# The order of attention units and the place of their loads in a fused transformer layer on one core

## The chip, the cores and the metric

The kernel runs on one core of a Trainium2 chip. The metric is the device time of one execution in microseconds (us), and lower is better. Five engines run side by side, each with its own instruction stream, and meet at semaphores: TensorE (PE; PEld is its weight load), VectorE (DVE), ScalarE (ACT), GpSimd (POOL) and SyncE (SP, which here only issues DMAs and waits).

## The reference

One layer of a diffusion transformer over 1024 latent tokens and 256 context tokens, width 1024: a modulated norm, one combined input projection, two groups of attention heads side by side, an output projection, and then a mixture of experts (top 8 of 64, and one shared expert). The part at issue is attention. There are four differential heads, each with two score matrices, whose probabilities are subtracted, and eight grouped query heads, which share two key heads.

```python
def mix_groups(dq, dk, dv, gq, gk, gv, lam, lam_init, subln_g):
    o1 = attend(dq[:, :, :, 0], dk[:, :, :, 0], dv, sc)
    o2 = attend(dq[:, :, :, 1], dk[:, :, :, 1], dv, sc)
    o_diff = rmsnorm(o1 - lam.astype(o2.dtype) * o2, subln_g) * (1.0 - lam_init)
    o_gqa = attend(gq, gk, gv, sc)
    return jnp.concatenate([o_diff.reshape(b, L, -1), o_gqa.reshape(b, L, -1)], axis=-1)
```

`attend` is plain softmax attention of 1024 queries over 1280 keys (context and latent); all is float32.

## The kernel before

Three functions follow one another on all engines: `front` (modulation, projections), `attention`, `tail` (output projection, routing, experts). Queries and keys are split into a high and a low part; `front` writes them to HBM scratch (`q_scratch`, `k_scratch`), and `attention` loads them from there. Key heads 0 to 7 are the differential ones, 8 and 9 the grouped ones.

**Units.** Attention is cut into 24 units. A differential unit ("d", block, head) takes 512 queries of one head, with 8 score rows of 128 queries (two for each tile, as there are two score matrices). A grouped unit ("g", tile, key head) takes 128 queries of the four query heads that share a key head, with 4 rows. The order (L716 to L719) is: four differential, eight grouped, four differential, eight grouped. `row0[u]` counts the rows ahead of unit u.

**The pipeline.** While unit u is in its body, ten steps kt of turning probabilities (`tr`, L1084) and multiplying them by the values (`pv`, L1098 and L1102), TensorE also scores the rows of unit u+1 (`qk`, L1070) at steps that `ROW_AT` names; at the end of the body it scores row 0 of unit u+2 and, for a differential one, row 1 as well. Each row goes from TensorE to VectorE (`rowmax`, L975) to ScalarE (`exp`, L933). The rows of unit 0 and the first of unit 1 are scored ahead of the loop (L1116 to L1119). Grouped rows lie at columns 0 and 1280 of the score banks, so both parities use the third bank, and the last 256 columns of a row wait for the row before (L1067). At the end of a body ScalarE copies the sum (`out_o`, L948) and TensorE turns it back (`back`) in step 1 of the next body; then VectorE's `finish(u)` (L999) scales it into one of two output tiles `ob`. From unit 2 on `finish` waits for the store of unit u-2 (L1002). The product of step 1 waits for `finish` (L1096). For a differential unit Pool does half of the subtractions (`mix`, L881).

**Loads and stores.** Pool issues, in its own order, four query loads a unit (`load_q`, double buffered, after the rows of the unit two before are scored) and one load for each key head (640 KB). Heads 0 and 1 lie in `k_first`, loaded near the end of `front` together with the first queries; the other eight lie in `k_high_low`. `s_k` has one semaphore for each pair of key heads. SP issues, in its own order: the load of the sub-norm's gain; then it waits for all five key semaphores (L843); then six transfers for later stages (L845 to L850: constants, 257 KB of pads, 4 MB of zeros from HBM to HBM, the first 3 MB of w_out); then the output stores of the units one after the other, each when its unit is ready. Ahead of unit 18's turn it loads the rest of w_out and the first output tile (L853 to L859).

Of the kernel before, what the change touches and what calls it, by code (L numbers as in the profile page):

```python
# [19 lines left out]
P = 128  # L20
D = 1024
KD = D // P
SEQ, CTX = 1024, 256
NT, NC = SEQ // P, CTX // P
# [3 lines left out]
DH, GH, GKV = 4, 8, 2  # L28
# [58 lines left out]
def load_queries(eng, s_q, dst, q_d, h0, nh, at, w):  # L87

    for part in range(2):
        for r in range(2):  # L90
            eng.dma_start(dst[r * HD:(r + 1) * HD, part, 0:nh * w].rearrange("p (c n) -> p c n", n=w),
                          q_d[part, h0:h0 + nh, :, at:at + w].rearrange("c d n -> d c n")).then_inc(s_q, 16)


def load_key(eng, s_k, dst, k_d, hd):

    eng.dma_start(dst, k_d[hd].rearrange("e d n -> (e d) n")).then_inc(s_k[hd // 2], 16)


def front(b, a, ident, rows, nlam, mhalf, vv, first, s_q, s_k, q_d, k_d):  # L100
# [10 lines left out]
    units = [(c, t) for c in range(len(CH)) for t in ORDER if t >= NC or CH[c][2] != "q"]  # L111
    NU = len(units)
    heads = {"k": 8, "kv": 2, "v": 0, "q": 8}
    turned = [n for n in range(NU) if heads[CH[units[n][0]][2]]]
    normed = [n for n in range(NU) if CH[units[n][0]][3] == 8]
    last_of = [max(n for n in range(NU) if units[n][0] == c) for c in range(len(CH))]
    first_of = [min(n for n in range(NU) if units[n][0] == c) for c in range(len(CH))]
# [35 lines left out]
    with ExitStack() as ph:  # L153
# [11 lines left out]
        qk = b.sb(ph, "qk_rows", [P, 2, 512])  # L165
# [74 lines left out]
        @block.gpsimd  # L240
        def _(pool):
            nc.gpsimd.memset(mhalf[:, 0:16], -0.5)
            nc.gpsimd.memset(mhalf[:, 16:32], EPS).then_inc(s_pool, 1)
            pool.wait_ge(s_pool, 1)
            n = [1]

            def rstd(dst, src, w, done):
                nc.gpsimd.tensor_tensor(dst, src, mhalf[:, 16:16 + w], ALU.add).then_inc(s_pool, 1)
                n[0] += 1
                pool.wait_ge(s_pool, n[0])  # L250
                nc.gpsimd.tensor_tensor(dst, dst, mhalf[:, 0:w], ALU.pow).then_inc(done, 1)

            for i, t in enumerate(XORDER):
                if i == 4:
                    pool.dma_start(rt[:], a["k_rope"][CTX:].rearrange("(t p) a d -> p t a d", p=P)).then_inc(s_rt, 16)
                    pool.dma_start(gain[:, 0], a["q_norm_g"].broadcast_to([P, HD])).then_inc(s_rt, 16)
                    pool.dma_start(gain[:, 1], a["k_norm_g"].broadcast_to([P, HD])).then_inc(s_rt, 16)
                pool.wait_ge(s_sq, i + 1)
                rstd(ssq[:, 1, t:t + 1], ssq[:, 0, t:t + 1], 1, s_rx)
            for r, g in ((G1, "g_post_mix"), (A2, "g_pre_ffn"), (G2, "g_post_ffn")):  # L260
                pool.dma_start(rows[:, r], a[g].broadcast_to([P, D])).then_inc(s_gains, 16)
            for m in range(NU):
                if m in normed:
                    nh = heads[CH[units[m][0]][2]]
                    pool.wait_ge(s_hv, n_normed(m) + 1)
                    rstd(hss[:, m % 2, 1, 0:nh], hss[:, m % 2, 0, 0:nh], nh, s_rr)
            qf, kf = first
            pool.wait_ge(s_wl, len(CH) * KD)
            pool.wait_ge(s_mt, NM)
            pool.wait_ge(s_mm, EARLY + 4 * (NM - EARLY))  # L270
            for hd in range(2):
                load_key(pool, s_k, kf[:, hd], k_d, hd)
            ready = turned.index(first_of[-1] + 4)
            for u in range(2):
                pool.wait_ge(s_st[u], stored(u, ready))
            load_queries(pool, s_q[0], qf, q_d, 0, 2, 0, 512)

        @block.sync
        def _(sp):
# [427 lines left out]
def attention(b, a, ident, rows, nlam, mhalf, moe, wa, vv, first, s_q, s_k, q_d, k_d, o_d, rows_d, slot_d, y2_d, early, s_od):  # L707
# [4 lines left out]
    NKH = 10  # L712
    QB = 4
    KEEP = 5

    units = []  # L716
    for qb in range(SEQ // (QB * P)):
        units += [("d", qb, p) for p in range(DH)]
        units += [("g", qb * QB + t, h) for t in range(QB) for h in range(GKV)]  # L719
    NU = len(units)  # L720

    def n_rows(u):
        return 8 if units[u][0] == "d" else 4
# [22 lines left out]
    def mixes(u, pool):  # L746
        return [i for i in range(4) if (i in ON_POOL) == pool] if units[u][0] == "d" else []
# [30 lines left out]
    with ExitStack() as ph:  # L778
        qf, kf = first
# [42 lines left out]
        S = psS[:].rearrange("p b n -> p (b n)")  # L822

        def key(hd):
            return kf[:, hd] if hd < 2 else k2[:, hd - 2]

        def pT(u, kt):
            return psS[:, 5 + turn_bank(u, kt)]
# [2 lines left out]
        @block.sync  # L831
        def _(sp):
            def store(u):
                kind, t, p = units[u]
                sp.wait_ge(s_o, u + 1)
                if kind == "d":
                    sp.dma_start(o_d[t * QB * P:(t + 1) * QB * P, p * DIFF_V:(p + 1) * DIFF_V].rearrange("(t p) n -> p t n", p=P),
                                 ob[:, u % 2].rearrange("p (t n) -> p t n", n=P)).then_inc(s_od[u % 2], 16)
                else:
                    sp.dma_start(o_d[t * P:(t + 1) * P, 512 + p * 256:512 + (p + 1) * 256], ob[:, u % 2, 0:256]).then_inc(s_od[u % 2], 16)  # L840

            sp.dma_start(sg[:], a["subln_g"].broadcast_to([P, DIFF_V])).then_inc(s_g, 16)
            for w in s_k:  # L843
                sp.wait_ge(w, 32)
            sp.dma_start(rows_d, rows[0:1].rearrange("p r n -> p (r n)")).then_inc(s_later, 16)  # L845
            sp.dma_start(slot_d, a["k_pads"]).then_inc(s_later, 16)
            sp.dma_start(y2_d[0:SEQ, :], a["k_zeros"]).then_inc(s_later, 16)
            sp.dma_start(first_row[:], a["k_first"].broadcast_to([P, E])).then_inc(s_later, 16)
            sp.dma_start(token[:], a["k_token"]).then_inc(s_later, 16)
            sp.dma_start(wa[:], a["w_out"][0, 0:wa.shape[1] * P, :].rearrange("(k p) n -> p k n", p=P)).then_inc(s_later, 16)  # L850
            last_diff = max(u for u in range(NU) if units[u][0] == "d")
            for u in range(NU):
                if u == last_diff + 3:  # L853
                    sp.wait_ge(s_s, row0[last_diff + 1])
                    sp.dma_start(w_rest[:], a["w_out"][0, wa.shape[1] * P:, :].rearrange("(k p) n -> p k n", p=P)).then_inc(s_rest, 16)
                    for w in s_od:
                        sp.wait_ge(w, (DH + GKV) // 2 * 16)
                    sp.dma_start(o_first[:], o_d[0:P, :]).then_inc(s_of_tile, 16)
                    sp.dma_start(x_first[:], a["tokens"][CTX:CTX + P, :]).then_inc(s_xr, 16)  # L859
                if u >= 1:  # L860
                    store(u - 1)
            store(NU - 1)
            sp.wait_ge(s_later, 96)
            sp.wait_ge(s_before, 16)
# [7 lines left out]
        @block.gpsimd  # L872
        def _(pool):
            def load_q(u):
                kind, t, p = units[u]
                if u >= 2:
                    pool.wait_ge(s_s, row0[u - 1])
                w, h0, nh, at = (512, 2 * p, 2, t * 512) if kind == "d" else (P, 2 * DH + 4 * p, 4, t * P)
                load_queries(pool, s_q[u % 2], (qf, qs)[u % 2], q_d, h0, nh, at, w)

            def mix(u, i):  # L881
                n = n_mix[u] + i
                m = n_mixp[u] + mixes(u, True).index(i)
                B = pb[:, i % 2]
                A = pr[:, u % 2, i]
                pool.wait_ge(s_c, n + 1)
                nc.gpsimd.tensor_scalar(B, B, cs[:, n % 4, 1:2], None, ALU.mult).then_inc(s_cs, 1)
                pool.wait_ge(s_cs, m + 1)
                nc.gpsimd.tensor_tensor(A, A, B, ALU.add).then_inc(s_mixp, 1)

            def rstd(u):
                pool.wait_ge(s_ov, n_diff[u] + 1)
                nc.gpsimd.tensor_tensor(ms[:, 2], ms[:, 1], mhalf[:, 0:4], ALU.pow).then_inc(s_or, 1)

            load_key(pool, s_k, key(2), k_d, 2)
            load_q(1)
            load_key(pool, s_k, key(3), k_d, 3)
            for i in mixes(0, True):
                mix(0, i)
            for hd in range(4, NKH):  # L900
                load_key(pool, s_k, key(hd), k_d, hd)
            nc.gpsimd.memset(ones[:], 1.0)
            pool.dma_start(before[:], a["k_before"]).then_inc(s_before, 16)
            for u in range(1, NU + 2):
                if u + 1 < NU:
                    load_q(u + 1)
                if u >= 2 and units[u - 2][0] == "d":
                    rstd(u - 2)
                if u < NU:
                    for i in mixes(u, True):  # L910
                        mix(u, i)
# [144 lines left out]
        def _(pe):  # L1056
# [59 lines left out]
            for r in range(n_rows(0)):  # L1116
                qk(0, r)
            qk(1, 0)
            qk(1, 1)  # L1119

            def second_row_late(u):
                return units[u][0] == "g"
# [1134 lines left out]
```

## Time and profile before

| what | us |
|---|---|
| median of three runs | 2174.56 (2169.73 to 2176.85) |
| span of the profiled execution | 2171.7 |
| projections and what is ahead of them | 0 to 372.2 |
| attention | 372.2 to about 889 |
| output projection, routing, experts, sum | about 889 to 2171.7 |

| engine | busy us of the span | share |
|---|---|---|
| PE | 1988.6 | 92% |
| PEld | 1487.5 | 68% |
| DVE | 1574.7 | 73% |
| ACT | 1351.4 | 62% |
| POOL | 942.6 | 43% |

The shares are means over stages that differ. The mean granted clock of TensorE is 0.971 of full speed; a value of 0.50 in a window is 1.2 GHz, 1.00 is 2.4 GHz. In a row of the timeline the first number is the start in us from the span's start, the second the length, and the bracket tells how long the engine was idle before it and what released it.

### The profile page before, as it was taken

To read this page: it belongs to the slowest core of one execution; us is meant where nothing else is said; L and a number is where in the kernel's file an instruction comes from. 1 tells how busy PE (TensorE), PEld (TensorE's weight loads), DVE (VectorE), ACT (ScalarE), POOL (GpSimd) and SP (SyncE) were. 2 spreads that over 40 slices of the span, in tenths; PEclk is the share of its full clock that TensorE was granted. 3 is DMA by queue.
4 is the path that set the end of the run, shared out by engine and by line. 5 is a ranking of instruction groups with operands and counts; after the bars stand their busy time and mean duration, and the time that the engine had idled before them with its cause. 6 is when DMAs were issued, how large, how long until landed. Compare 5 with 4: busy or idle time off the path is not lost.

```text
span 2171.7 us, 36325 instructions
## 1 busy us (share of the span) xinstructions
PE 1988.6 (92%) x9592; PEld 1487.5 (68%) x9592; DVE 1574.7 (73%) x2206; ACT 1351.4 (62%) x1952; POOL 942.6 (43%) x869
## 2 busy tenths in 40 slices
PE   4899998888988899989889999999999999999993
PEld 2676666555656566676548888888877888888881
DVE  3752374685556655465539999999988999999985
ACT  2421121555656556423338998999878999899982
POOL 1000011661135410044435666666656666666663
PEclk8999998799999999999999999999999999999997
DMA  7464346732122121397249998889999977789957
GB/s 266 140 181 141 98 145 160 218 80 42 40 50 41 40 78 30 113 192 155 80 129 320 327 368 285 244 259 330 354 333 351 343 234 229 217 233 366 287 147 260
DMA packets 162652, 429.18 MB, mean 198 GB/s; under 512 B 26993, under 2 KB 82033, under 8 KB 137889
## 3 DMA queue, kind: packets, MB, share of 16 engines
q1 hardware_dynamic: 92818, 294.36, 38.0%
q0 software_dynamic: 60048, 116.89, 24.2%
q10 hardware_dynamic: 9712, 16.99, 2.7%
q8 instruction: 41, 0.67, 0.1%
q14 instruction: 33, 0.27, 0.0%
HBM read 360.83 MB, written 96.26 MB: 210 GB/s over the span
## 4 chain that ended last, share of the span: by engine, by line
PE 43%; DMA 7%; DVE 3%; issue 2%; ACT 2%; ACTq 1%; POOL 0%; SPq 0%; DVEq 0%; POOLq 0%
PE ps_d L2099 11%; PE ps_r L2082 7%; PE ps_r L2084 7%; PE ps_r L2083 7%; DMA w_experts<-in_w_exp_down 5%; PE ps_y L2072 3%; PE ps_y L2001 2%; PE ps_g L2020 2%; PE ps_d L2039 1%; DMA x_in<-in_tokens 1%; PE ps_g L2106 1%; ACT w_gate_up_high L1612 1%; ACTq L1321 1%; DVE w_gate_up_low L1844 1%; PE ps_d L2001 1%
## 5 line engine op out<-in xcount | busy, mean ns | idle before, releaser
L1844 DVE TENSOR_TENSOR w_gate_up_low<-w_experts,w_gate_up_high 128x1024 fp32r<-128x1024 f32 x416 | 489.3, 1217 | 20.1 <-ACT w_gate_up_high L1612 20.0
L1612 ACT ACTIVATE w_gate_up_high<-w_experts 128x1024 fp32r x416 | 416.6, 1050 | 38.0 <-SPq L1366 17.4
L2082 PE MATMUL ps_r<-w_gate_up_high,gatheredT_high 128*128 128x512 f32 x832 | 335.2, 403 | 5.5 <-DVE gatheredT_low L1850 5.4
L1501 POOL DMA_INDIRECT y_scratch<-e_y,e_target_index x104 | 281.4, 2705 | 108.5 <-POOL e_target_index L1497 93.0
L2084 PE MATMUL ps_r<-w_gate_up_high,gatheredT_low 128*128 128x512 f32 x832 | 326.1, 392 | 0.0
L2083 PE MATMUL ps_r<-w_gate_up_low,gatheredT_high 128*128 128x512 f32 x832 | 324.2, 390 | 0.0
L975 DVE TENSOR_REDUCE neg_max<-ps_scores 128x1 f32<-128x1280 f32 x128 | 190.2, 1490 | 182.5 <-PE ps_scores L1070 182.4
L1879 DVE TENSOR_TENSOR w_down_low<-w_experts,w_down_high 128x2048 fp32r<-128x2048 f32 x103 | 236.0, 2292 | 44.8 <-ACT w_down_high L1637 44.1
L1487 POOL DMA_INDIRECT gathered<-h_scratch,e_gather_index x106 | 197.2, 1860 | 95.2 <-POOL e_gather_index L1484 90.1
L1637 ACT ACTIVATE w_down_high<-w_experts 128x2048 fp32r x103 | 198.0, 1923 | 36.1 <-issue 36.1
L933 ACT ACTIVATE probs<-ps_scores,neg_max 128x1280 f32<-128x1280 f32 x96 | 127.5, 1329 | 102.1 <-DVE neg_max L975 102.0
L1084 PE MATMUL ps_scores<-ident,probs 128*128 128x128 f32 x960 | 149.4, 283 | 38.0 <-ACT probsT L942 21.6
L2082 PEld LDWEIGHTS ps_r<-w_gate_up_high,gatheredT_high 128*128 128x128 f32 x832 | 156.6, 188 | 38.4 <-issue 9.4
L2084 PEld LDWEIGHTS ps_r<-w_gate_up_high,gatheredT_low 128*128 128x128 f32 x832 | 156.4, 188 | 34.3
L1084 PEld LDWEIGHTS ps_scores<-ident,probs 128*128 128x128 f32 x960 | 108.3, 143 | 101.4 <-ACT probsT L942 61.9
L2083 PEld LDWEIGHTS ps_r<-w_gate_up_low,gatheredT_high 128*128 128x128 f32 x832 | 157.0, 189 | 29.8 <-issue 0.2
L942 ACT ACTIVATE probsT<-ps_scores 128x512 f32<-128x512 f32 x192 | 112.5, 594 | 89.6 <-PE ps_scores L1084 89.6
L681 PE MATMUL ps_chunk<-w_in_high,hT_high 128*128 128x512 f32 (+1 forms) x368 | 143.9, 391 | 9.0 <-DVE hT_low L522 7.3
L1658 ACT ACTIVATE e_y<-ps_d 128x512 f32<-128x512 f32 x208 | 122.3, 592 | 38.6 <-PE ps_d L2099 37.4
L2099 PE MATMUL ps_d<-w_down_high,e_actT_high 128*128 128x512 f32 x416 | 137.9, 413 | 1.9 <-DVE e_actT_low L1868 1.8
L681 PE MATMUL ps_chunk<-w_in_high,hT_low 128*128 128x512 f32 (+1 forms) x368 | 136.9, 372 | 0.0
L681 PE MATMUL ps_chunk<-w_in_low,hT_high 128*128 128x512 f32 (+1 forms) x368 | 136.6, 371 | 0.0
(294 smaller groups left out, 3824.1 us busy)
## 6 DMA issues: line engine op xcount, KB each, us to landing
w_experts<-in_w_exp_gate SPq DMA_DIRECT2D x64, 1024.0 KB, 9.4
w_experts<-in_w_exp_up SPq DMA_DIRECT2D x64, 1024.0 KB, 13.0
w_experts<-in_w_exp_down SPq DMA_DIRECT2D x64, 1024.0 KB, 17.3
w_mod_later<-in_w_mod ACTq DMA_DIRECT2D x32, 512.0 KB, 3.7
w_mod_first<-in_w_mod SPq DMA_DIRECT2D x4, 2048.0 KB, 15.4
w_in_raw<-in_w_in SPq DMA_DIRECT2D x32, 256.0 KB, 3.6
values<-in_tokens SPq DMA_DIRECT2D x10, 512.0 KB, 11.3
k_high_low<-k_scratch POOLq DMA_DIRECT2D x8, 640.0 KB, 7.2
```

The costliest lines, as they stand in the source:

```text
L681: last = nc.tensor.matmul(psC[:, n % 4, 0:w], H[:, k, tok], W[:, m % WR, 0:w], start=(k + i == 0), stop=(k == KD - 1 and i == 2))
L1084: last = nc.tensor.transpose(pT(u, kt)[:, j * P:(j + 1) * P], pr[:, u % 2, j, kt * P:(kt + 1) * P], ident[:])
L1487: pool.indirect_dma_start(xg[u][:], None, h2_d, bass.IndirectOffsetOnAxis(ap=gi[u][:, 0:1], axis=0), bounds_check=SEQ - 1, oob_is_err=Fals ...
L1501: pool.indirect_dma_start(y_d[u], bass.IndirectOffsetOnAxis(ap=si[u][:, 0:1], axis=0), ye[u][:], None, bounds_check=SEQ + P - 1, compute_o ...
L1612: act.activation(split_slice(eH, j), raw_slice(ring, slot, j), ACT.Copy).then_inc(X["wH"], 1)
L1637: act.activation(dh[:].rearrange("p k n -> p (k n)"), ring[:, ds(slot, 1), 4096:6144].rearrange("p o n -> p (o n)"), ACT.Copy).then_inc(X[ ...
L1844: nc.vector.tensor_tensor(split_slice(eL, j), raw_slice(ring, slot, j), split_slice(eH, j).bitcast(F32), ALU.subtract).then_inc(X["wL"], 1)
L1879: nc.vector.tensor_tensor(dl[:].rearrange("p k n -> p (k n)"), ring[:, ds(slot, 1), 4096:6144].rearrange("p o n -> p (o n)"), dh[:].rearra ...
L2082: nc.tensor.matmul(psR[:], xH[:, k], eH[:, k], start=(k == 0), stop=False)
L2083: nc.tensor.matmul(psR[:], xH[:, k], eL[:, k], start=False, stop=False)
L2084: last = nc.tensor.matmul(psR[:], xL[:, k], eH[:, k], start=False, stop=(k == KD - 1))
L2099: last = nc.tensor.matmul(psD[:, h], A[:, k], W[:, k, h * 512:(h + 1) * 512], start=(j + k == 0), stop=(j + k == 3))
```

## The change

The first eight grouped units (tiles 0 to 3) come first, then all eight differential units, then the other eight grouped ones. So the loads near the end of the projections become the queries of grouped unit 0 (four heads, 128 columns) and key heads 8 and 9, which now lie in `k_first`; the eight differential key heads lie in `k_high_low` and are loaded two at a time in Pool's turns u = 1 to 4, each time behind the queries of unit u+1. Row 1 of unit 1 is no longer scored ahead. The wait ahead of the first output tile's load is for units 0 to 11.

```diff
@@ front, gpsimd
-            for hd in range(2):
-                load_key(pool, s_k, kf[:, hd], k_d, hd)
-            ready = turned.index(first_of[-1] + 4)
+            ready = turned.index(first_of[3]) + 1
             for u in range(2):
                 pool.wait_ge(s_st[u], stored(u, ready))
-            load_queries(pool, s_q[0], qf, q_d, 0, 2, 0, 512)
+            load_queries(pool, s_q[0], qf, q_d, 2 * DH, 4, 0, P)
+            for hd in range(2 * DH, 2 * DH + GKV):
+                load_key(pool, s_k, kf[:, hd - 2 * DH], k_d, hd)
@@ attention
-    units = []
-    for qb in range(SEQ // (QB * P)):
-        units += [("d", qb, p) for p in range(DH)]
-        units += [("g", qb * QB + t, h) for t in range(QB) for h in range(GKV)]
+    grouped = [("g", t, h) for t in range(NT) for h in range(GKV)]
+    differential = [("d", qb, p) for qb in range(SEQ // (QB * P)) for p in range(DH)]
+    units = grouped[:QB * GKV] + differential + grouped[QB * GKV:]
     NU = len(units)
+    TILE0 = QB * GKV + DH
...
-            return kf[:, hd] if hd < 2 else k2[:, hd - 2]
+            return k2[:, hd] if hd < 2 * DH else kf[:, hd - 2 * DH]
...
-                        sp.wait_ge(w, (DH + GKV) // 2 * 16)
+                        sp.wait_ge(w, TILE0 // 2 * 16)
...
-            load_key(pool, s_k, key(2), k_d, 2)
             load_q(1)
-            load_key(pool, s_k, key(3), k_d, 3)
-            for i in mixes(0, True):
-                mix(0, i)
-            for hd in range(4, NKH):
-                load_key(pool, s_k, key(hd), k_d, hd)
             nc.gpsimd.memset(ones[:], 1.0)
             pool.dma_start(before[:], a["k_before"]).then_inc(s_before, 16)
             for u in range(1, NU + 2):
                 if u + 1 < NU:
                     load_q(u + 1)
+                if u <= DH:
+                    for hd in (2 * u - 2, 2 * u - 1):
+                        load_key(pool, s_k, key(hd), k_d, hd)
...
             for r in range(n_rows(0)):
                 qk(0, r)
             qk(1, 0)
-            qk(1, 1)
```

## Rows read from the trace of the kernel before

**Rows 1.** Windows: busy us (instructions) of five engines; clock, DMA share, GB/s.
```profile
404.00:408.00 4.00, 3.54 (x13) 2.74 (x11) 1.28 (x1) 1.79 (x4) 0.06 (x1) 0.50 1.11 419
...
540.00:560.00 20.00, 19.54 (x113) 12.39 (x112) 9.85 (x10) 11.97 (x20) 2.75 (x5) 1.00 0.27 53
658.00:665.00 7.00, 6.31 (x19) 4.39 (x18) 2.38 (x5) 3.17 (x7) 2.49 (x1) 0.51 0.05 19
```

**Rows 2.** Timeline, start of attention: start, length, engine, line, operation [idle <- releaser].
```profile
369.24 0.51 SPq L309 DMA_DIRECT2D q_scratch<-turned_low  x1
...
372.42 4.61 PE L1070 MATMUL ps_scores<-k_first,q_first 128*128 128x512 f32 x12 [5.06 <-PEq L153]
...
377.41 1.33 ACT L933 ACTIVATE probs<-ps_scores,neg_max 128x1280 f32<-128x1280 f32 x1 [9.33 <-DVE neg_max L975]
...
383.01 1.33 ACT L933 ACTIVATE probs<-ps_scores,neg_max 128x1280 f32<-128x1280 f32 x1 [2.78 <-DVE neg_max L975]
...
397.71 3.31 POOL L97 DMA_DIRECT2D k_high_low<-k_scratch  x6
...
401.69 1.05 PE L1084 MATMUL ps_scores<-ident,probs 128*128 128x128 f32 x4
```

**Rows 3.** Timeline of ScalarE: the copies that end units 0 to 4.
```profile
430.29 0.60 ACT L948 ACTIVATE oT_head<-ps_out 128x512 f32<-128x512 f32 x1
...
458.13 0.59 ACT L948 ACTIVATE oT_head<-ps_out 128x512 f32<-128x512 f32 x1
...
485.98 0.59 ACT L948 ACTIVATE oT_head<-ps_out 128x512 f32<-128x512 f32 x1
...
511.31 0.59 ACT L948 ACTIVATE oT_head<-ps_out 128x512 f32<-128x512 f32 x1
...
527.97 0.59 ACT L948 ACTIVATE oT_head<-ps_out 128x512 f32<-128x512 f32 x1
```

**Rows 4.** Timeline, one grouped body among its like (560.17 to 576.27).
```profile
560.17 0.59 ACT L948 ACTIVATE oT_head<-ps_out 128x512 f32<-128x512 f32 x1
...
562.95 0.17 DVE L1003 RECIPROCAL row_scale<-row_sum 128x4 f32<-128x4 f32 x1
...
565.28 1.08 PE L1102 MATMUL ps_out<-probsT,values 128*64 128x512 f32 x4
...
568.32 1.43 PE L1070 MATMUL ps_scores<-k_high_low,q_first 128*128 128x512 f32 x6
...
570.04 2.45 POOL L91 DMA_DIRECT2D q_first<-q_scratch  x4 [13.65 <-PE ps_scores L1070]
...
576.27 0.59 ACT L948 ACTIVATE oT_head<-ps_out 128x512 f32<-128x512 f32 x1
```

**Rows 5.** Timeline of SP: first and last of its bundle, and the first output store.
```profile
412.66 0.24 SPq L845 DMA_DIRECT2D rows_scratch<-mod_rows  x1
...
415.33 0.56 SPq L850 DMA_DIRECT2D w_out_ahead<-in_w_out  x1
...
446.84 0.38 SPq L837 DMA_DIRECT2D o_scratch<-o_tile  x1
```

**Rows 6.** Windows while the bundle moves; the last two columns are DMA share and GB/s.
```profile
418.00:422.00 4.00, 4.00 (x23) 3.18 (x23) 1.84 (x2) 2.70 (x6) 3.92 (x2) 1.00 1.55 508
...
426.00:430.00 4.00, 4.00 (x16) 2.38 (x15) 3.93 (x5) 2.10 (x3) 0.79 (x2) 1.00 0.06 14
...
442.00:444.00 2.00, 2.00 (x9) 1.04 (x8) 1.97 (x3) 1.51 (x2) 1.92 (x2) 1.00 0.38 135
```

**Rows 7.** Landing times: six key loads (L97, from 397.7), then seven grouped stores (L840).
```profile
DMA to landing us min/median/max: 4.4/7.2/12.1
...
DMA to landing us min/median/max: 1.7/1.7/1.9
```

**Rows 8.** DMA queues in 430 to 444 (q1 is SP's, q0 Pool's): packets, MB, share.
```profile
q1 hardware_dynamic: 885, 3.13, 74.0%
q0 software_dynamic: 576, 1.05, 25.5%
```

## The prediction

> **What bounds the kernel now.** I read the windows by stage first, for what the change can reach: the last few us of the projections and all of attention. In the grouped units TensorE is busy 19.5 us of 20 at the full clock (2.4 GHz) [rows 1], so there the pitch is TensorE's own work. In the differential units it shares the pace with the chain scores, row maximum, exponential. Then I read the timeline of the start of attention: the last query store is issued at 369.24, the first scores start at 372.42, and until 401.69 (the first turn of probabilities, L1084) the engines only fill the pipeline: 29.3 us in which a row's maximum and exponential wait for one another [rows 2]. Third, the copies of the finished output (oT_head, L948), one a unit: their distance is the length of a unit's body. A differential unit followed by another takes 27.84 us (458.13 to 485.98), one followed by a grouped unit 25.33, a grouped unit right after a differential one 16.66 [rows 3], a grouped unit among its like 16.10 (560.17 to 576.27) [rows 4]. Last I read SP's issues and the DMA windows, because the change moves what SP waits for [rows 5, 6].
>
> **Part 1, the loads inside the projections: nothing.** Pool issues four query loads (128 KB each in place of 256 KB) and the two grouped keys where it issued two keys, and no longer loads queries at 356. Pool was free for them at 339.9; the last key is then issued at 343 and in by 355 even at the slowest landing, 12.1 [rows 7], 17 us ahead of the first scores at 372.42 [rows 2]. They share engines with SP's query stores there, each of which has two projection chunks before its buffer is wanted. If this cover failed, a store of 2.5 us would come late once: 1 to 2 us. The end of the projections hangs on the last rotary step and the last two stores, and neither moves. In attention Pool starts with load_q(1) at once; its memset and the load of "before" come earlier, beside idle Pool time.
>
> **Part 2, the fill: about -11.9 us.** Before, eight rows of unit 0 and two of unit 1 are scored ahead, and Pool mixes probabilities; now four and one. The first exponential starts at 377.41 and ends 1.33 later, at 378.74 [rows 2]; this stays, since it waits on the same things. Grouped rows share their third score bank, so the last 256 columns of a row wait for the exponential of the row before: the chain is serial, 1.49 (maximum) + 1.33 (exponential) + about 0.5 (two 256-column products at half clock, from 4.61 us for twelve products of 5120 columns [rows 2]) + 0.15 of handing over = 3.5 us a row. Three more rows end at 389.2, and the last piece of unit 1's row makes the first turn start at 389.8 in place of 401.69. A differential pair came in 5.6 us (377.41 to 383.01 [rows 2]), so the bounds for three rows are 8.4 and 10.8: -11.0 to -14.0. The second row of unit 1, no longer scored ahead, is scored after the first turn as in every other grouped body.
>
> **Part 3, the first body: about -9.5 us.** Unit 0 took 430.29 - 401.69 = 28.6 us; a grouped one takes 16.10 at full clock. The granted clock was 0.50 at 404 to 408 although TensorE was busy [rows 1], and a TensorE-bound body feels that: each us at 1.2 GHz costs half a us. Nothing to 11 us of it costs 0 to 5.5; I take 3, so 19.1 us: -9.5, bounds -7 to -12.5.
>
> **Part 4, the order: about +13.7 us.** Both orders hold the same 24 units. The new one has two more bodies of differential followed by differential (because the first unit, counted in part 3, is now a grouped one), and one less of differential-to-grouped and of grouped-after-differential: 2 x 27.84 - 25.33 - 16.66 = +13.7 [rows 3]. The way from grouped to differential is paid once in both. TILE0 makes SP await six stores a parity in place of three, but still in unit 18, when units 0 to 11 are long stored: nothing. Parts 2 to 4 together: -7.7 us.
>
> **Part 5, the keys one pair a unit: a new wait, about +28.4 us.** This is where the change is paid. Before Pool had issued the last keys by 401 (six from 397.71 [rows 2]), SP woke at 412.66 and issued the zeros, the row constants and the 3 MB of w_out by 415.9; the first output store came much later, at 446.84 [rows 5], when the queue was empty. Now heads 6 and 7 are loaded in Pool's turn u = 4, behind load_q(5), which waits for the last row of unit 3. SP waits for ALL keys before its bundle, and **every output store stands behind that wait on SP**. VectorE's finish of unit 2 (L1001 to L1002) needs the store of unit 0, as the output tile has two buffers, and it runs early in unit 3's body. Count from the start of unit 2's body, which is the copy of unit 1's output:
> - the last row of unit 3 is scored and Pool released at 570.04 - 560.17 = +9.87 [rows 4]
> - four query loads, 2.45, and the first key, 0.6 (six took 3.31 [rows 2]): the second key is issued at +12.9
> - landing 6.0: the quickest of the six keys took 4.4, the median 7.2 [rows 7]: keys are in at +18.9
> - SP's bundle, in the transfer order of its queue: from 412.6 to 430 it moved pads, zeros, then only small rows at 14 GB/s; w_out, issued at 415.33, moved only from 430 [rows 5, 6] and ended about 443.5, where the engines' share falls to 0.38 [rows 6]. In that stretch SP's queue had 74.0% of the transfers and Pool's queries 25.5% [rows 8]; now no queries go out meanwhile, so 3.13 MB at the 300 to 330 GB/s of both together is 10 us in place of 13.5: 27.4, and 31 without that saving
> - the store's own landing, 1.7 [rows 7], plus its start: store of unit 0 in at about +48.9 (30 after the keys)
> - needed: unit 3's body starts at +16.1; finish starts 2.78 into it and the product L1102, which waits for it, 5.11 into it; the finish takes 0.6, so 1.6 us are slack [rows 4]: +20.5
> The stall is 48.9 - 20.5 = **28.4 us**. Bounds: with keys landing after 4.4 and the bundle in 28.5, 25.3; with 12.1 and 33, 37.5. Queued behind VectorE's wait are the row maxima of unit 4, thus ScalarE's exponentials and TensorE's turns; TensorE stops at L1102 for want of the freed output bank, and Pool's next loads wait for its rows. Later waits for stores find them landed: they pay nothing again.
>
> The Trainium skill has two rules here. "DMA: Bandwidth & Descriptors", section "Queues, rings and completion order", says an engine takes turns between queues packet by packet; by it w_out alone goes at the full rate, the 27.4 above. The trace agrees in the shares of rows 8. The same section says completion within one issuing engine is not first in, first out; a store that used this would land early, which is the first rival below. The trace speaks for order here: w_out waited 15 us behind the rest [rows 5, 6].
>
> **Part 6, the clock after the stall: about +3.5 us.** TensorE idles some 25 us, then has 11 us of unit 3's body left, all its own work. After pauses the trace shows half clock for 7 us (658 to 665) and, in the fill, up to 412 [rows 1]: 4 to 11 us at 1.2 GHz, 2 to 5.5 us lost.
>
> **Sum.** -11.9 - 9.5 + 13.7 + 28.4 + 3.5 = +24.2 us. The profiled span of 2171.7 becomes 2195.9; the median of the runs stands 2.9 above that span, so 2198.8 us, 1.1% slower. The rest (output projection, experts) starts later and is otherwise as it was. A measurement of this kernel can tell about 0.3%, 6.5 us, from no change.
>
> **The rivals.**
> - *The store slips past the bundle* (the other side). If SP's 128 KB store lands 1.7 after its issue though 7 MB are queued ahead, it is in at 18.9 + 3.3 + 1.7 = +23.9, and VectorE waits 3.4 us, with little loss of clock. Then -7.7 + 3.4 = -4.3: 2170.3; and if the first body also runs at full clock, -7.3: 2167. It decides for faster once the store comes under +22 and the first body loses under 2 us. Against it: w_out did not pass the zeros [rows 5, 6]. Chance 0.07, of which 0.03 is faster.
> - *The wait is not there at all*, because SP is released before unit 2: -7.7, 2166.9. It needs the last keys in by about unit 0; Pool's wait for row scores puts them two units later. Chance 0.02.
> - *A shorter stall*: zeros and w_out drain without contention in 20 us, not 30: +14, 2188.6. For it: at 418 to 422 the engines moved 508 GB/s [rows 6]. Against: the 4 us of small rows at 14 GB/s [rows 6]. Chance 0.10.
> - *A longer stall*: keys and queries compete as in the 12.1 us landing [rows 7], or the zeros go slower: +33 to +38, 2208 to 2213. Chance 0.13.
> - *The forecast*, 2192 to 2206: 0.68.
>
> **How the numbers follow.** The likeliest case gives 2198.8. The low end takes in most of the shorter stall, 2188; the high end is the upper bounds of part 5 with the rest as taken, 2211. Faster: 0.03 + 0.02 = 0.05. Same: 0.04 and a bit of the shortest stalls, 0.05. Slower: 0.90.
>
> **What would show it.** Right: the first turn L1084 near 390 and the first copy L948 near 409; copies then 16.1 apart until unit 3, whose body is some 48 us long; SP's first issue after the last key lands, about 444; a VectorE idle of about 28 us before L1003, put down to a store to o_scratch; a granted clock of 0.5 in and just after it; then 27.8 for six differential bodies in a row. Wrong: stores landing in 2 us while w_out is moving; VectorE's wait absent; grouped bodies other than 16.1 before unit 3; or a change beyond attention's last copy.

## The result, and the profile after

The changed kernel takes 2197.48 us (median of four runs, 2191.74 to 2203.39), the kernel before 2173.23 (four runs, 2169.73 to 2176.85): a ratio of 1.0101, with a 95% interval of 1.0079 to 1.0124. It is 1.0% slower. The forecast was 2198.8 (2188 to 2211). The profiled span grew from 2171.7 to 2193.5 us, by 21.8.

Line numbers of attention are three lower than before: the scores are L1067 (was L1070), the turns L1081 (L1084), the grouped product L1099 (L1102), the copy that ends a unit L945 (L948), the first step of `finish` L1000 (L1003).

First the waits of the changed kernel from 372 to 500 (who waited for whom: us in total, times, longest). In the trace of before neither engine waits for a store of the output between 372 and 520.

```profile
DVE row_scale L1000 <- DMA o_scratch<-o_tile: 27.2, 1, 27.2
PE ps_out L1099 <- DVE o_tile L1009: 25.6, 1, 25.6
```

One wait of VectorE, 27.2 us, put down to a store to `o_scratch`; one of TensorE behind it, 25.6 us. Now the copies that end the units, from ScalarE's timeline: units 0, 1, 2, 3 and the last.

```profile
412.09 0.59 ACT L945 ACTIVATE oT_head<-ps_out 128x512 f32<-128x512 f32 x1
...
428.18 0.59 ACT L945 ACTIVATE oT_head<-ps_out 128x512 f32<-128x512 f32 x1
...
444.27 0.59 ACT L945 ACTIVATE oT_head<-ps_out 128x512 f32<-128x512 f32 x1
...
487.99 0.59 ACT L945 ACTIVATE oT_head<-ps_out 128x512 f32<-128x512 f32 x1
...
909.61 0.60 ACT L945 ACTIVATE oT_head<-ps_out 128x512 f32<-128x512 f32 x1 [1.28 <-PE ps_out L1099]
```

Units 1 and 2 take 16.09 us each, as grouped bodies did in rows 4; unit 3 takes 43.72, which is 27.6 too long; no later body differs from its like in the kernel before by more than 2.3 us. The timeline of SP and of what it holds up, from 447 on:

```profile
447.73 0.24 SPq L845 DMA_DIRECT2D rows_scratch<-mod_rows  x1
...
450.40 0.47 SPq L850 DMA_DIRECT2D w_out_ahead<-in_w_out  x1
...
450.91 40.89 SPq L840 DMA_DIRECT2D o_scratch<-o_tile  x4
474.29 0.18 DVE L1000 RECIPROCAL row_scale<-row_sum 128x4 f32<-128x4 f32 x1 [27.16 <-DMA o_scratch<-o_tile]
...
475.07 1.98 PE L1099 MATMUL ps_out<-probsT,values 128*64 128x512 f32 x4 [25.63 <-DVE o_tile L1009]
```

In rows 5 SP began its bundle at 412.66, and the first store went out long after it, at 446.84. Here the bundle starts at 447.73 and the store of unit 0, ready since about 415.5, is issued right behind it, at 450.91. The landing time of that one store, and then of the two keys issued at 440.5 and 441.0:

```profile
DMA to landing us min/median/max: 23.3/23.3/23.3
...
DMA to landing us min/median/max: 4.2/5.4/6.5
```

23.3 us, where rows 7 have 1.7 to 1.9 for such a store: it lands at 474.2, and VectorE goes on at 474.29. And what the DMA engines did meanwhile (windows; columns as in rows 1):

```profile
456.00:460.00 4.00, 0.00 (x0) 0.00 (x0) 0.00 (x0) 0.00 (x0) 0.00 (x0) 0.50 1.36 442
460.00:464.00 4.00, 0.00 (x0) 0.00 (x0) 0.00 (x0) 0.00 (x0) 0.00 (x0) 0.50 0.16 55
...
468.00:472.00 4.00, 0.00 (x0) 0.00 (x0) 0.00 (x0) 0.00 (x0) 0.00 (x0) 0.50 1.02 421
```

No compute engine does anything; the queue moves the zeros (to about 461), then little until about 464 (55 GB/s in the second window, which still holds the zeros' end: the small rows), then w_out at 421 GB/s, then the store. Which transfer a window belongs to is inferred from the order of issue; experiments 3 and 4 test it by taking the large ones out. It is the sequence of rows 6, with the store at its end.

### The profile page after: what moved, and what is told of

Same layout as the page of the kernel before. It is cut to its first block, busy times and chain, and to the rows that moved or that the text cites. A ratio compares the mean times of both kernels' runs of the same rounds, so it can differ in the third digit from the quotient of the medians.

```text
span 2193.5 us, 36328 instructions
## 1 busy us (share of the span) xinstructions
PE 1990.6 (91%) x9592; PEld 1485.8 (68%) x9592; DVE 1579.7 (72%) x2206; ACT 1350.9 (62%) x1952; POOL 944.2 (43%) x869
## 4 chain that ended last, share of the span: by engine, by line
PE 42%; DMA 7%; issue 3%; DVE 3%; ACT 2%; ACTq 1%; SPq 0%; POOL 0%; DVEq 0%; POOLq 0%
PE ps_d L2095 10%; PE ps_r L2078 7%; PE ps_r L2080 7%; PE ps_r L2079 7%; DMA w_experts<-in_w_exp_down 5%; PE ps_y L2068 3%; PE ps_y L1997 2%; PE ps_g L2016 2%; PE ps_d L2035 2%; PE ps_d L1997 1%; ACT w_gate_up_high L1608 1%; DMA x_in<-in_tokens 1%; ACTq L1317 1%; PE ps_g L2102 1%; DVE w_gate_up_low L1840 0%
## 5 line engine op out<-in xcount | busy, mean ns | idle before, releaser
L1081 PE MATMUL ps_scores<-ident,probs 128*128 128x128 f32 x960 | 149.1, 283 | 35.1 <-ACT probsT L939 18.2
L1081 PEld LDWEIGHTS ps_scores<-ident,probs 128*128 128x128 f32 x960 | 108.4, 143 | 96.8 <-ACT probsT L939 55.0
```

What stands on the lines that cost most here:

```text
L1081: last = nc.tensor.transpose(pT(u, kt)[:, j * P:(j + 1) * P], pr[:, u % 2, j, kt * P:(kt + 1) * P], ident[:])
```

## The experiments

All ratios are to the kernel before, run on the same chip in the same job. Two theories stood against each other: that VectorE waited for a store which stood behind SP's key wait and its bundle, and that the grouped-first order, or the late bundle as such, costs by itself.

**1. Two stores ahead of the bundle.** The changed kernel; SP awaits the keys and issues the six transfers in its turn 3, behind the stores of units 0 and 1. (The cut is abridged: "..." stands for the wait and the six transfers.)

```diff
-            for w in s_k: ...                # key wait and six transfers, ahead of the loop
             for u in range(NU):
+                if u == 3:
+                    for w in s_k: ...
                 if u == last_diff + 3:
```

> The changed kernel, with one edit: SP stores units 0 and 1 first, and only then waits for the keys and issues its bundle. Theory (VectorE waited for stores that stood behind SP's key wait and the bundle): the 27.16 us idle of VectorE before L1000 is gone, unit 3's body falls from 43.71 us to about 16.1, and the store of unit 2, now behind the bundle, lands near 475, ahead of its use near 481. Time about 27.5 us below the changed kernel's 2197.5: 2170, 0.1 to 0.2% under the kernel before. Rival (the grouped-first order costs by itself, through query loads that the bundle slows or through the keys): unit 3's body stays well above 16, or the lost time shows up in units 4 and 5, and the time stays over 2180.

Measured: 2182.29 us (12 runs) against 2179.36, ratio 1.0004 (0.9986 to 1.0022). The time is back to that of before, not under it: some 21 us came back of the 27.5 forecast. VectorE's wait is gone and unit 3's body is 16.10. But unit 4's body is 21.95 us in place of 16.10, as the copies of units 3 and 4 show, and behind them the wait list of 456 to 496 says why:

```profile
456.20 0.59 ACT L946 ACTIVATE oT_head<-ps_out 128x512 f32<-128x512 f32 x1
...
478.15 0.60 ACT L946 ACTIVATE oT_head<-ps_out 128x512 f32<-128x512 f32 x1
```
```profile
PE ps_scores L1068 <- DMA q_first<-q_scratch: 4.4, 1, 4.4
```

TensorE waited for queries. Their landing time, of the four loads for unit 6, issued from 450 on beside the bundle:

```profile
DMA to landing us min/median/max: 13.0/16.5/20.8
```

Up to 20.8 us, where the grouped units' queries had a median of 2.8 in the kernel before (28 loads from 521.7 on). Units 5 and 7 are 1.0 and 1.6 us longer as well. So the main theory holds, and its rival has a part: while the bundle moves, a query load can land later than a short unit can wait. The store of unit 2, now behind the bundle, landed 26.2 us after its issue, at 473.3, ahead of its use. In the changed kernel this price was hidden, since Pool issued no queries during the stall.

**2. All differential keys at once.** The changed kernel; Pool loads the eight keys right behind the first queries.

```diff
             load_q(1)
+            for hd in range(2 * DH):
+                load_key(pool, s_k, key(hd), k_d, hd)
...
-                if u <= DH:
-                    for hd in (2 * u - 2, 2 * u - 1):
-                        load_key(pool, s_k, key(hd), k_d, hd)
```

> The changed kernel, with one edit: Pool loads all eight differential keys right behind the first queries, not a pair a unit. Theory (the late pair of keys is what made SP late): SP's bundle goes out near 392 instead of 447.7 and is done by about 422, the stores of units 0 and 1 land by 434, VectorE finds no wait, unit 3's body is 16.1 us, and the time is 2170 (plus up to 3 us if the queries of units 2 and 3, loaded beside the bundle, land late: needed near 408 and 424). Rival (the stall comes from the bundle moving at all while short grouped units run, whenever it is): a stall of similar size, 20 us or more, moves to units 1 or 2, and the time stays over 2190.

Measured: 2172.43 us (10 runs) against 2179.36, ratio 0.9978 (0.9957 to 1.0000). The bundle and the first store, from SP's timeline, and the store's landing time:

```profile
389.60 0.24 SPq L845 DMA_DIRECT2D rows_scratch<-mod_rows  x1
...
411.85 32.52 SPq L840 DMA_DIRECT2D o_scratch<-o_tile  x3
```
```profile
DMA to landing us min/median/max: 7.2/7.2/7.2
```

The store of unit 0 still lands behind the bundle's end, 7.2 us after its issue, but 24 us ahead of its use. No body is longer than its kind, from the first copy on: the attention of this run takes 506.7 us from the first scores to the last copy, before it took 514.0, in the changed kernel 536.6. This undoes one thing alone, the spacing of the keys, and the whole loss is gone. That is the changed order without the stall: 7.3 us less than before, where parts 2 to 4 of the prediction have 7.7. The queries of unit 3, issued at 402 to 404 beside the bundle, took 11.4 to 15.6 us, but landed in time; those of unit 2 had gone out ahead of it and took 3.8 to 4.2.

**3 and 4. What of the bundle costs what.** The changed kernel, with the 4 MB of zeros issued in SP's turn 8 instead; then with the 3 MB of w_out moved there too (the cut shows the first).

```diff
-            sp.dma_start(y2_d[0:SEQ, :], a["k_zeros"]).then_inc(s_later, 16)
+                if u == 8:
+                    sp.dma_start(y2_d[0:SEQ, :], a["k_zeros"]).then_inc(s_later, 16)
```

> The changed kernel, with the 4 MB of zeros taken out of the bundle and issued in SP's turn 8, behind the store of unit 6. Theory (the store waits for what is ahead of it in SP's queue): the zeros took about 12 us of the 26.6 between the last key's landing and the store's, so VectorE's idle falls from 27.2 to about 15, unit 3's body to about 31.5, the time to about 2185. Rival (the wait is for the keys, or for the queue as such, not for the bytes): the idle stays at 25 or more.

> As the one with the zeros later, and the 3 MB of w_out with them: ahead of the store stand only the row constants and pads. Theory: w_out took another 9 us; small rows keep about 5 to 6 of the 26.6, so the idle of VectorE is 5 to 7 us (of which some 4 are the key wait alone), unit 3's body 20 to 23, the time about 2176. If VectorE's idle is under 2, the key wait by itself cost nothing and the bundle all; if it stays above 12, the bundle's bytes are not the cause.

VectorE's wait for the store, from the wait lists of 372 to 520, first without the zeros, then without both:

```profile
DVE row_scale L1001 <- DMA o_scratch<-o_tile: 14.1, 1, 14.1
```
```profile
DVE row_scale L1001 <- DMA o_scratch<-o_tile: 5.9, 1, 5.9
```

27.2, 14.1, 5.9: the zeros are worth 13.1 us of the wait, w_out 8.2, and 5.9 remain. Of these the late keys by themselves are little: in the second run SP begins its bundle at 441.18, 0.6 us after VectorE's wait begins (5.92 ahead of 446.46); the other 5.3 are the issuing of the small transfers and of the store (at 443.22) and its landing, 3.1. Unit 3's body follows, 43.7, 30.3, 22.1. One execution each: spans of 2186.7 and 2176.8 us. The store waits for what is ahead of it in SP's queue, and the pieces add up one by one: from SP's first issue to the store's landing it is 26.5, 13.4 and 5.1 us.

**5. All differential units first.** The kernel before, with another order; the first output tile's load two turns later and with its own count.

```diff
-    units = []
-    for qb in range(SEQ // (QB * P)):
-        units += [("d", qb, p) for p in range(DH)]
-        units += [("g", qb * QB + t, h) for t in range(QB) for h in range(GKV)]
+    units = [("d", qb, p) for qb in range(SEQ // (QB * P)) for p in range(DH)]
+    units += [("g", t, h) for t in range(NT) for h in range(GKV)]
...
-                if u == last_diff + 3:
+                if u == last_diff + 5:
...
-                        sp.wait_ge(w, (DH + GKV) // 2 * 16)
+                        sp.wait_ge(w, (2 * DH + GKV) // 2 * 16)
```

> The kernel before with all eight differential units first and then all sixteen grouped ones; loads and keys as before, the first output tile's load moved two turns later. Theory (the order is worth what the bodies' lengths say): the start of attention is unchanged (first copy near 430.3, or 57.9 us after the first scores); two more bodies of 27.85 and eight more of 16.10 take the place of one way from grouped to differential (19.88, 26.42, 28.38) and of one way back (25.33, 16.66), which makes 443.7 us from the first copy to the last in place of 456.1: 12.5 us less, ratio 0.994, 7 us below the changed kernel without its stall. Rival (the transitions' prices belong to the places, not to the kinds): under 5 us of gain.

Measured: 2160.75 us (6 runs) against 2177.83, ratio 0.9923 (0.9899 to 0.9947), the fastest of all. First and last copy:

```profile
428.68 0.60 ACT L946 ACTIVATE oT_head<-ps_out 128x512 f32<-128x512 f32 x1
...
874.75 0.60 ACT L946 ACTIVATE oT_head<-ps_out 128x512 f32<-128x512 f32 x1 [1.28 <-PE ps_out L1100]
```

446.1 us between them, forecast 443.7 (the expectation says "eight more of 16.10"; the lists of units give three more, which make 443.4), before 456.1: 10.1 less. The eighth differential body took 27.45 in place of the 25.33 of rows 3. From the first scores to the last copy it is 11.4 us less. The runs say 11 to 22 us less; what the part above 11.4 us is was not tried.

**6 and 7. The late bundle in the old order.** Run 6 was to send the bundle out near 448 by placing the last key pair behind Pool's first mix of unit 1.

```diff
             for i in mixes(u, True):
                 mix(u, i)
+                if u == 1 and i == 0:
+                    for hd in range(NKH - 2, NKH):
+                        load_key(pool, s_k, key(hd), k_d, hd)
```

> The kernel before, its order kept, with the last pair of keys (8 and 9) loaded behind Pool's first mix of unit 1, so that SP's bundle goes out about when it does in the changed kernel, near 448. Theory (a late bundle costs only where short units need the output tile within its 27 us): unit 0's store lands near 476, VectorE needs it in unit 3's body at about 491, the queries of unit 4 land by 475 for a use near 480; no stall, time as before within 0.2%. Rival (a late bundle costs some 20 us in any order): over 2190.

It missed its aim: Pool makes that mix in unit 0's body, so that the bundle went out at 415.14, 2.5 us later than in rows 5. Its ratio, 0.9988 (0.9970 to 1.0006), says nothing on the question. Run 7 holds SP itself:

```diff
             for w in s_k:
                 sp.wait_ge(w, 32)
+            sp.wait_ge(s_s, row0[2] + 6)
```

> The kernel before, its order and its loads kept, with SP's bundle held back until the sixth row of unit 2 is scored, near 448, ahead of all output stores as in the changed kernel. Theory (a late bundle costs only where short units need the output tile, or the queries, within its 27 us): unit 0's store lands near 475 and VectorE needs it in unit 3's body near 491; unit 4's queries, issued near 454, land by 476 for a use near 480; all bodies keep their lengths, time as before within 0.3%. Rival (a bundle at that time costs 20 us in any order): body of unit 3 over 45 us, time over 2190.

Measured: 2179.58 us (10 runs) against 2177.54, ratio 1.0008 (0.9987 to 1.0029). The bundle went out at 440.33, not near 448: 25 us later than in run 6, and 7.4 us earlier than in the changed kernel. The start of the bundle and the first store in SP's timeline, the store's landing time, and VectorE's use of the tile in unit 3's body:

```profile
440.33 0.24 SPq L846 DMA_DIRECT2D rows_scratch<-mod_rows  x1
...
443.56 74.19 SPq L837 DMA_DIRECT2D o_scratch<-o_tile  x4
```
```profile
DMA to landing us min/median/max: 24.9/24.9/24.9
```
```profile
484.81 0.18 DVE L1004 RECIPROCAL row_scale<-row_sum 128x4 f32<-128x4 f32 x1
```

The store takes about as long as in the changed kernel, 24.9 us against 23.3, and lands at 468.5; VectorE wants it at 484.8, 16 us later, and does not wait. By these numbers a bundle 7.4 us later still would have left some 9 us (an estimate). The bodies of units 1 and 2 are 27.8 and 27.9 us as in rows 3. Unit 3's is 27.68 in place of 25.33, but it is 27.31 in run 6 as well, whose bundle went out at 415. The late bundle that costs 27.6 us among units of 16.1 us costs nothing that the time shows among units of 27.8.

## Why the prediction was right, point by point

| term | forecast | measured | from |
|---|---|---|---|
| start of the first scores | 0 | +0.6 | 372.42 to 372.98 |
| part 2, fill to the first turn | -11.9 | -10.8 | 29.27 to 18.46 |
| part 3, first body | -9.5 | -8.0 | 28.60 to 20.65 |
| part 4, order | +13.7 | +13.8 | first copy to last, less the stall: 456.1 to 469.9 |
| parts 5 and 6, stall and clock | +28.4 + 3.5 | +27.6 | 43.7 less 16.1 |
| after the last copy | 0 | -1.4 | 21.8 less the sum above, 23.2 |

The mechanism and its main term held. That the sum came so close, +24.2 forecast against 24.25 us between the medians, is in part luck. The profiled spans differ by 21.8, and there parts 2 and 3 gave 2.6 us less than forecast, while parts 5 and 6 cost 4.3 less; the two misses offset each other. These are also single traces: from the first scores to the first copy it took 34.8 to 39.1 us in the five traces that start with grouped units, and 51.9 to 57.9 in the four that start with differential ones, so that the sizes of parts 2 and 3 are known to a few us only.

**Part 1** held. The keys and queries were in by 351, the last query store went out at 369.79 (369.24 in rows 2).

**Part 2** was near, but its -10.8 lies outside its bounds of -11.0 to -14.0: the three rows took 11.2 us (378.18 to 389.38), where the bounds had at most 10.8, a number that no row gives. The rows of the fill, from ScalarE's and TensorE's timelines, the first three exponentials and the first turn:

```profile
378.18 1.33 ACT L930 ACTIVATE probs<-ps_scores,neg_max 128x1280 f32<-128x1280 f32 x1 [9.54 <-DVE neg_max L972]
...
381.72 1.33 ACT L930 ACTIVATE probs<-ps_scores,neg_max 128x1280 f32<-128x1280 f32 x1 [2.12 <-DVE neg_max L972]
...
385.55 1.33 ACT L930 ACTIVATE probs<-ps_scores,neg_max 128x1280 f32<-128x1280 f32 x1 [2.41 <-DVE neg_max L972]
...
391.44 1.05 PE L1081 MATMUL ps_scores<-ident,probs 128*128 128x128 f32 x4
```

The serial chain through the shared third bank is there, at 3.54 us for the first row, when the granted clock was 1.00 (378 to 380) as its last 256 columns began, and 3.83 for the others, at 0.50; I had 3.5 for all. At 0.50 those columns took 0.80 us a row, where I had 0.5.

**Part 3** had the right cause and was 1.5 us short: 20.65 us for the body, forecast 19.1; in experiments 1 to 4 the same body took 19.1 to 19.4. All lie in the range given, 16.1 to 21.6. In the changed kernel the granted clock was still 0.66 at 396 to 400 and 0.91 at 400 to 404.

**Part 4** came out to 0.1 us, but that closeness is luck, since its lengths are not exact: the first differential body after grouped ones took 26.21 us (28.38 in the kernel before) and the last one 27.21 (24.92 in the kernel before; rows 3 have 25.33 for the other such body). The two differences, -2.2 and +2.3, cancel. Experiment 5 has only the second of them, its 27.45, and that is most of the 2.4 us by which its 446.1 missed 443.7. The last differential body before grouped ones takes 24.9 to 27.7 us in the nine traces, with no cause shown.

**Part 5** is the term that decides, and its steps came in the order worked out: Pool released 9.87 us after unit 1's copy (438.05), the second key issued at +12.84 (forecast +12.9), the keys in at +19.4 (+18.9), the store in at +46.0 (+48.9). The 28.4 is net of the 1.6 us of slack, so what answers it is TensorE's stop, 25.6 us; VectorE's wait of 27.2 is that and the 1.6 (the prediction's own numbers make it 30.0, not the "about 28" among its signs). The step mis-sized is the bundle's drain, 26.6 us from the keys' landing to the store's in place of 30. w_out alone moved at 421 GB/s, not at the 300 to 330 of both queues together: 7.4 us for its 3.13 MB in place of 10. Experiment 1 took the stall away and 2 took its cause away, 3 and 4 split it into its bytes, 7 showed that it needs the short units.

**Part 6** was too high: TensorE stopped for 25.6 of the 27.6 us, so clock and all else cost 2.0, against 3.5. The granted clock was 0.50 until 479, 0.88 in the us from 479 to 480 and 1.00 in the next: full some 4 us after the restart at 475.07, the short end of the 4 to 11 that I allowed.

**The rivals.** That the store would slip past the bundle did not happen, in any of the runs: with the bundle ahead, a store took 23.3 us to land, 24.9 (experiment 7), 26.2 (experiment 1) and 7.2 (experiment 2, issued late in the bundle). The Trainium skill ("DMA: Bandwidth & Descriptors", section "Queues, rings and completion order") says both that an engine takes descriptors in ring order and that completions within one issuing engine need not come in order; in these four landings only the first half showed. The stall was neither of the other sizes: the drain of 26.6 lies between the 20 of the shorter one and the forecast's 30. The high end of the range is not what its words give: the upper bound of part 5, 37.5, with the rest as taken makes 2207.9, not 2211. What the forecast did not have is the second price of a late bundle, the queries of experiment 1. It took no time from the changed kernel, but a repair that only moved two stores would have run into it, and did.

## What to carry to other kernels

When a load is moved later, follow the waits that other queues make on its semaphore: here a pair of keys that nobody needed for about another 170 us (by the order of the units) held back SP, and with it 7 MB and then the output stores that free a double buffer. A queue that serves in order and carries both large transfers ahead of need and small stores that someone waits for should issue the large ones while the next small one is still far from its deadline, and the deadline is the length of the unit times the number of buffers. Compare orders of unlike units by the lengths of the bodies between their copies, grouped by what comes next: it gave the order's worth here within some 3 us, the spread of the bodies next to a change of kind, and pointed to a better one.

## What the runs showed of the hardware that I had not expected

One queue alone moved w_out faster, 421 GB/s, than it and Pool's queries of 2 KB pieces together moved. A window of the kernel before, in the stretch of rows 8 (columns as in rows 1):

```profile
434.00:438.00 4.00, 2.83 (x14) 1.70 (x13) 3.67 (x6) 2.66 (x5) 0.00 (x0) 1.00 1.11 319
```

319 GB/s for the two, at about the same share of the engines' time (1.11 here, 1.02 alone). The packets of this window (434 to 438), and of 462 to 470 in experiment 1, where the queries are grouped ones, by queue (q1 is SP's, q0 Pool's: packets, MB, share):

```profile
q1 hardware_dynamic: 214, 0.88, 77.0%
q0 software_dynamic: 215, 0.40, 34.0%
```
```profile
q1 hardware_dynamic: 680, 2.73, 90.4%
q0 software_dynamic: 677, 0.33, 20.9%
```

The two queues moved almost the same number of packets, 214 and 215, 680 and 677 (696 and 618 in 408 to 416 of experiment 2): here the turns that the prediction spoke of can be seen, which the shares of rows 8 alone do not show. So what Pool's queue took from SP's went by the size of Pool's packets: beside 1.9 KB ones w_out moved at 220 GB/s, beside 0.5 KB ones at 341. Query loads of 128 KB, issued beside the bundle, landed after 13.0 to 20.8 us (experiment 1), against 2.5 to 5.3 in 515 to 640 of the kernel before, although they were on a queue of their own: it is the engines that are shared, not only the queue. The Trainium skill says the same ("DMA: Bandwidth & Descriptors", section "Issuing engines are not separate DMA queues"): all issuers run on the same 16 engines and interleave.
